# Paged attention of a hybrid decoder: the next sequence's value pages asked for two, two, two and two in the slots of a period instead of two, four and two

## The chip, the core and the metric

One core of a Trainium2 chip runs the whole program. TensorE (PE) multiplies, VectorE (DVE) and ScalarE (ACT) work on the results, GpSimd (POOL) splits weights, SyncE (SP) issues transfers; ScalarE issues transfers too. The transfers run on 16 DMA engines. The metric is the device time of one execution in microseconds (us); lower is better.

## The reference

One inference step of a small decoder: a retention layer with its MLP, then a forgetting-attention layer (FoX) with its MLP, over 512 prompt tokens with 16 meta tokens and over 8 running sequences of 8 new tokens. The change touches only the attention of the 8 running sequences. Each has 1024 past keys and values in 8 pages of 128 rows, found by a page table in a pool in HBM; a page holds 16 heads of 64 floats a row, 512 KB.

```
k_past = cache_k[page_table].reshape(DB, P, FOX_HEADS, FOX_DH)
v_past = cache_v[page_table].reshape(DB, P, FOX_HEADS, FOX_DH)
s = concat(q . k_past, q . k_new) * FOX_SCALE + cum_new[q] - cum_k     # cum: running sum of log forget
p = softmax(where(mask, s, MASK_VALUE))
o = p[..., :P] . v_past + p[..., P:] . v_new
```

## The kernel before, in words

All matrix work is done in float32 or in split float32 (high and low parts). Weights stream through two slots; the layers before and after the attention are bound by PE. The order of work is written out by hand, each engine has its own program, and semaphores join them.

The attention runs from about 1290 to 1557 us of the span. It is one loop over b = 0 to 8 (nine periods), each of four slots i = 0 to 3. A slot of period b does one pair of prompt heads and query block, number j = 4b + i - 2, and a part of the work of sequences b and b - 1:

- Keys. SP asks for key pages (`k_page`, line 683), four transfers of 128 KB a page, into a ring of four buffers (NKS = 4). A buffer is asked for anew when VectorE has turned (transposed) the page in it (line 2390, `turn_page`, into `k_page_t`, four buffers). VectorE turns two pages in every slot, in its program's order, between the row maxima and the sums of the prompt's pair. PE takes two turned pages at a time (`pair_scores`, line 1318).
- Scores and softmax of sequence b - 1 end in slots 0 and 1 of period b: new keys' scores, maxima (line 2397), the exponential on ScalarE (line 1830), transposes on PE (line 1348), and the copies of the transposed probabilities: tokens 512 and on by VectorE, the first 512 and the new ones by ScalarE (lines 1835 and 1838).
- Values. PE multiplies pages 0 to 3 of sequence b - 1 in slot 2 of period b and pages 4 to 7 in slot 3 (`page_values`, line 1363, in page order, 8 instructions a page). It waits there for v_in and then counts v_used. The ring has eight buffers (NVS = 8), the whole of one sequence.
- Requests of values. The first eight pages are asked for by SP. All later ones, 56 of 512 KB, are asked for by ScalarE (line 1846, in `v_next`): it loads the page number from the page table, waits until the page in that buffer has been used, and starts the transfer. Page p of sequence b goes out in period b: pages 0 and 1 in slot 2, pages 2 to 5 in slot 3, pages 6 and 7 in slot 0 of the period after. Each request stands in ScalarE's program behind the activations of its slot, and what follows on ScalarE waits until it is issued.

The names in the rows: `probs_t` is the copy of the prompt pair's transposed probabilities (line 1824, with line 1826 for the meta tokens), which PE's products of line 1293 and 1298 (`values`) wait for; line 1252 is a part of the prompt pair's scores.

Of the kernel before, what the change touches and what calls it, by code (L numbers as in the profile page):

```python
# [206 lines left out]
def program(nc, io):  # L207
    ctx = ExitStack()
    with ctx:
# [354 lines left out]
        def pair_at(b, i):  # L564

            return 4 * b + i - 2

        def live(j):

            return 0 <= j < NPAIR  # L570
# [205 lines left out]
        def _(pe):  # L776
# [123 lines left out]
            def norm_sum(f, n):  # L900

                pe.wait_ge(sq_used, KT * (f + 1))
                a, w = (L0, SL2) if f == 3 else (0, SW)
                for i in range(4):
                    c = slice(a + w * i, a + w * i + w)
                    last = pe.matmul(PS[:, 4 * n.slot + i, HF:HF + w], ck("ones"), RR[:, c], start=False, stop=True,
                                     skip_group_check=True)
                if f == 0:
                    for w, (a, _) in enumerate(WINDOWS):
                        last = pe.matmul(PS[:, 4 * n.slot, HF + SW + w:HF + SW + w + 1], RR[:, a:a + P],  # L910
                                         ck("ones")[:, 0:1], start=False, stop=True, skip_group_check=True)
                last.then_inc(sums_ready, 1)
# [230 lines left out]
            def fox_sums(t):  # L1143

                normed(2)(t)
                if t == KT - 1:
                    pe.wait_ge(sq_used, KT * 3)
                    for hf in range(2):
                        pe.matmul(PS[:, 3 + 4 * hf, 0:HF], ck("ones"), RR[:, HF * hf:HF * hf + HF], start=True, stop=True)
                    for w, (a, _) in enumerate(WINDOWS):  # L1150
                        last = pe.matmul(PS[:, 3, HF + w:HF + w + 1], RR[:, a:a + P], ck("ones")[:, 0:1], start=False,
                                         stop=True, skip_group_check=True)
                    last.then_inc(sums_ready, 1)
# [309 lines left out]
        def _(act):  # L1463
# [343 lines left out]
            def exp(j, par):  # L1807
                n = keys_of(j % 4)
                act.wait_ge(mx_done, 2 * j + (2 if j % 4 == 3 else par + 1))
                act.activation(own_probs(par, n), score_cols(par, n), ACT.Exp, bias=NM[:, par:par + 1],  # L1810
                               accum_out=SM[:, par:par + 1]).then_inc(ex_done, 1)

            def normed_probs(j):
                act.wait_ge(inv_row, j + 1)
                n = keys_of(j % 4)
                for par in range(2):
                    x = own_probs(par, n)
                    act.activation(x, x, ACT.Copy, scale=RM[:, par:par + 1]).then_inc(pn_done, 1)

            def probs_copy(j):  # L1820
                m = P * (j % 4 + 1)
                for par in range(2):
                    act.wait_ge(pt_ready, 3 * j + par + 1)
                    act.activation(PTS[:, par, 0:m], PS[:, 4 + 2 * par, 0:m], ACT.Copy).then_inc(pt_evac, 1)
                act.wait_ge(pt_ready, 3 * j + 3)
                act.activation(PTM[:], PS[0:2 * NMETA, 7, 2 * P:3 * P], ACT.Copy).then_inc(pt_evac, 1)

            def exp_s(b):
                act.wait_ge(smx_done, b + 1)
                act.activation(PB[:], PS[:, 0:3, :].rearrange("p a n -> p (a n)")[:, 0:SK], ACT.Exp, bias=NM[:, 2:3],  # L1830
                               accum_out=SM[:, 2:3]).then_inc(sex_done, 1)

            def probs_copy_s(b):
                act.wait_ge(sp0_ready, b + 1)
                act.activation(PSM[:, 0:4, :], PS[:, 6, :].rearrange("p (t n) -> p t n", t=4), ACT.Copy) \
                    .then_inc(sp0_done, 1)
                act.wait_ge(spn_ready, b + 1)
                act.activation(PSN[:], PS[0:NSAMP, 2, 320:448], ACT.Copy).then_inc(spn_done, 1)

            def v_next(b, pages):  # L1840
                for p in pages:
                    vn = NPAGE * b + p + NVS
                    if 0 <= b < DB - 1:
                        page = act.value_load(PT1[0:1, vn:vn + 1], min_val=0, max_val=io["cache_v"].shape[0] - 1)
                        act.wait_ge(v_used, NPAGE * b + p + 1)
                        act.dma_start(VR[vn % NVS][:], v_pool[bass.ds(page, 1)].rearrange("o k f -> k (o f)")) \
                            .then_inc(v_in[vn % NVS], 16)

            act.wait_ge(k_stored, 48)
            for b in range(DB + 1):  # L1850
                for i in range(4):
                    j = pair_at(b, i)
                    if live(j - 1):
                        probs_copy(j - 1)
                    if live(j):
                        for par in range(2):
                            exp(j, par)
                        normed_probs(j)
                    if i == 0 and b > 0:
                        exp_s(b - 1)  # L1860
                    if i == 1 and b > 0:
                        probs_copy_s(b - 1)
                    if i == 2:
                        v_next(b - 1, (0, 1))
                    if i == 3:
                        v_next(b - 1, (2, 3, 4, 5))
                    if i == 0:
                        v_next(b - 2, (6, 7))
            for dst, src in out_v:
                act.dma_start(dst, src).then_inc(v_stored, 16)  # L1870
# [630 lines left out]
```

## Time and profile before

| what | value |
|---|---|
| time, median of 3 runs (lowest, highest) | 2012.95 us (2012.68, 2015.09) |
| span of the profiled execution (its only time) | 2016.3 us |
| busy share of the span: PE, DVE, ACT, POOL | 96%, 51%, 34%, 22% |
| DMA in the whole span | 239.11 MB, mean 119 GB/s |
| key pages asked for by SP, line 683 | 256 transfers of 128 KB, median 5.9 us to landing |
| value pages asked for by ACT, line 1846 | 56 transfers of 512 KB, median 8.3 us to landing |

The profiled execution is 3.3 us longer than the median of the runs. Times are counted from the start of the span. PE is busy for 96% of the whole, so a reader would look for gains there; the attention is the stretch where it is not. A row of a view of windows gives the length of the stretch, then for each engine its busy time and, in brackets, the instructions begun, the mean granted clock of PE (1.00 is 2.4 GHz, 0.50 is 1.2 GHz), the mean share of the 16 DMA engines that were at work (over 1 where transfers of two queues overlap on an engine), and the rate. A row of a timeline gives start and duration, the engine, line and operation, and in square brackets how long the engine stood idle before it and what ended that.

### The profile page before, as it was taken

To read this page: it belongs to the slowest core of one execution; us is meant where nothing else is said; L and a number is where in the kernel's file an instruction comes from. 1 tells how busy PE (TensorE), PEld (TensorE's weight loads), DVE (VectorE), ACT (ScalarE), POOL (GpSimd) and SP (SyncE) were. 2 spreads that over 40 slices of the span, in tenths; PEclk is the share of its full clock that TensorE was granted. 3 is DMA by queue.
4 is the path that set the end of the run, shared out by engine and by line. 5 is a ranking of instruction groups with operands and counts; after the bars stand their busy time and mean duration, and the time that the engine had idled before them with its cause. 6 is when DMAs were issued, how large, how long until landed. Compare 5 with 4: busy or idle time off the path is not lost.

```text
span 2016.3 us, 35504 instructions
## 1 busy us (share of the span) xinstructions
PE 1926.1 (96%) x14783; PEld 1775.5 (88%) x14783; DVE 1033.0 (51%) x1170; ACT 692.8 (34%) x898; POOL 440.1 (22%) x106
## 2 busy tenths in 40 slices
PE   7999999999999999999999999799997999999998
PEld 6969969969889999999999999655555999999998
DVE  4445245245436865555532535466665466646462
ACT  4132232232224325252531432243545332515241
POOL 2302312312303312121133233000000332121212
PEclk9999999999999999999999999998998999999999
DMA  5341441441243222222232221688998222322231
GB/s 162 126 155 55 137 142 68 137 140 63 101 167 95 84 70 99 84 83 83 98 94 64 65 84 44 206 242 242 286 282 247 85 84 68 101 84 86 80 104 47
DMA packets 197347, 239.11 MB, mean 119 GB/s; under 512 B 16418, under 2 KB 168354, under 8 KB 197026
## 3 DMA queue, kind: packets, MB, share of 16 engines
q1 hardware_dynamic: 175650, 183.27, 30.0%
q10 hardware_dynamic: 21488, 53.46, 8.0%
q8 instruction: 97, 1.59, 0.3%
q0 software_dynamic: 80, 0.52, 0.1%
q14 instruction: 32, 0.26, 0.0%
HBM read 210.77 MB, written 26.12 MB: 117 GB/s over the span
## 4 chain that ended last, share of the span: by engine, by line
PE 64%; issue 16%; DVE 6%; DMA 5%; POOL 4%; ACT 2%; SPq 2%; ACTq 1%; DVEq 0%; POOLq 0%
PE PS L801 12%; PE PS L802 11%; PE PS L803 11%; POOL w_lo L741 4%; PE PS L817 4%; PE PS L819 4%; PE PS L818 4%; DMA k_page<-in_cache_k 3%; PE PS L880 3%; PE PS L881 3%; PE PS L882 3%; SPq L683 1%; DVE k_page_t L2390 1%; PE PS L1363 1%; PE PS L1318 1%
## 5 line engine op out<-in xcount | busy, mean ns | idle before, releaser
L741 POOL TENSOR_TENSOR w_lo<-w_raw,w_hi 128x2048 fp32r<-128x2048 f32 (+2 forms) x101 | 438.9, 4346 | 1545.0 <-ACT w_hi L1468 1545.0
L1468 ACT ACTIVATE w_hi<-w_raw 128x2048 fp32r<-128x2048 f32 (+2 forms) x101 | 178.1, 1764 | 640.8 <-PE PS L803 415.5
L801 PE MATMUL PS<-hidden_hi,w_hi 128*128 128x296 f32 (+1 forms) x1024 | 304.4, 297 | 0.7 <-DVE hidden_tmp L2159 0.6
L803 PE MATMUL PS<-hidden_hi,w_lo 128*128 128x296 f32 (+1 forms) x1024 | 304.7, 298 | 0.0
L802 PE MATMUL PS<-hidden_lo,w_hi 128*128 128x296 f32 (+1 forms) x1024 | 304.2, 297 | 0.0
L801 PE MATMUL PS<-x_hi,w_hi 128*128 128x296 f32 (+1 forms) x896 | 269.9, 301 | 5.7 <-DVE x_lo L1918 2.8
L802 PE MATMUL PS<-x_lo,w_hi 128*128 128x296 f32 (+1 forms) x896 | 268.7, 300 | 0.0
L803 PE MATMUL PS<-x_hi,w_lo 128*128 128x296 f32 (+1 forms) x896 | 268.0, 299 | 0.0
L880 PE MATMUL PS<-w_hi,x_hi 128*128 128x256 f32 x800 | 225.8, 282 | 0.4 <-DVE fox_gate L2311 0.4
L882 PE MATMUL PS<-w_lo,x_hi 128*128 128x256 f32 x800 | 224.8, 281 | 0.0
L881 PE MATMUL PS<-w_hi,x_lo 128*128 128x256 f32 x800 | 224.6, 281 | 0.0
L801 PEld LDWEIGHTS PS<-hidden_hi,w_hi 128*128 128x128 f32 x1024 | 193.1, 189 | 1.6 <-issue 1.0
L802 PEld LDWEIGHTS PS<-hidden_lo,w_hi 128*128 128x128 f32 x1024 | 193.2, 189 | 0.0
L803 PEld LDWEIGHTS PS<-hidden_hi,w_lo 128*128 128x128 f32 x1024 | 192.6, 188 | 0.0
L801 PEld LDWEIGHTS PS<-x_hi,w_hi 128*128 128x128 f32 x896 | 169.6, 189 | 7.4 <-issue 3.5
L802 PEld LDWEIGHTS PS<-x_lo,w_hi 128*128 128x128 f32 x896 | 169.5, 189 | 0.3 <-issue 0.2
L803 PEld LDWEIGHTS PS<-x_hi,w_lo 128*128 128x128 f32 x896 | 169.4, 189 | 0.0
L880 PEld LDWEIGHTS PS<-w_hi,x_hi 128*128 128x128 f32 x800 | 150.5, 188 | 1.1 <-issue 1.0
L882 PEld LDWEIGHTS PS<-w_lo,x_hi 128*128 128x128 f32 x800 | 150.7, 188 | 0.0
L881 PEld LDWEIGHTS PS<-w_hi,x_lo 128*128 128x128 f32 x800 | 150.5, 188 | 0.0
L2159 DVE TENSOR_TENSOR hidden_tmp<-PS,inv_root 128x1184 f32<-128x1184 f32 (+1 forms) x32 | 44.0, 1374 | 178.2 <-PE PS L803 178.0
L1475 ACT ACTIVATE w_hi<-w_raw 128x2048 fp32r<-128x2048 f32 x24 | 46.1, 1919 | 196.6 <-DVE w_raw L2122 196.6
(306 smaller groups left out, 3883.4 us busy)
## 6 DMA issues: line engine op xcount, KB each, us to landing
w_raw<-in_w_mlp_up SPq DMA_DIRECT2D x32, 1024.0 KB, 5.3
w_raw<-in_w_mlp_down SPq DMA_DIRECT2D x32, 1024.0 KB, 5.0
k_page<-in_cache_k SPq DMA_DIRECT2D x256, 128.0 KB, 5.9
v_page<-in_cache_v ACTq DMA_DIRECT2D x56, 512.0 KB, 8.3
w_raw<-in_w_ret_in SPq DMA_DIRECT2D x24, 1024.0 KB, 5.4
sample_state<-in_state_ret SPq DMA_DIRECT2D x32, 512.0 KB, 5.6
out_state_ret_sample<-sample_state ACTq DMA_DIRECT2D x32, 512.0 KB, 4.3
w_raw<-in_w_ret_out SPq DMA_DIRECT2D x16, 512.0 KB, 3.4
```

The source lines that it names most:

```text
L741: pool.tensor_tensor(lo, raw, hi.bitcast(F32), ALU.subtract).then_inc(lo_done, 1)
L801: pe.matmul(o, wh[:, w], xh[:, t, cols], start=(t == 0), stop=False)
L802: pe.matmul(o, wh[:, w], xl[:, t, cols], start=False, stop=False)
L803: last = pe.matmul(o, wl[:, w], xh[:, t, cols], start=False, stop=(t == kt - 1))
L817: pe.matmul(o, wh[:, t], xh[:, t], start=first and t == 0, stop=False, skip_group_check=True)
L818: pe.matmul(o, wh[:, t], xl[:, t], start=False, stop=False, skip_group_check=True)
L819: last = pe.matmul(o, wl[:, t], xh[:, t], start=False, stop=(t == 3), skip_group_check=True)
L880: pe.matmul(o, XH[:, t, tok], wh[:, c], start=start, stop=False, skip_group_check=skip)
L881: pe.matmul(o, XL[:, t, tok], wh[:, c], start=False, stop=False, skip_group_check=skip)
L882: return pe.matmul(o, XH[:, t, tok], wl[:, c], start=False, stop=(t == KT - 1), skip_group_check=skip)
L1468: act.activation(part(WH[n.slot], n, kt), part(WR[n.slot], n, kt), ACT.Copy).then_inc(hi_done, 1)
L1475: act.activation(WH[n.slot][:], WR[n.slot][:], ACT.Copy).then_inc(hi_done, 1)
```

## The change

Inside the loop over b and i, only the place of three of the eight requests changes. Pages 2 and 3 stay in slot 3; pages 4 and 5 go from slot 3 to slot 0 of the next period; pages 6 and 7 go from there to slot 1. The first period in which a request is moved is b = 1 (from its slot 3 on), the last requests now go out in slot 1 of b = 8.

```diff
                     if i == 2:
                         v_next(b - 1, (0, 1))
                     if i == 3:
-                        v_next(b - 1, (2, 3, 4, 5))
+                        v_next(b - 1, (2, 3))
                     if i == 0:
+                        v_next(b - 2, (4, 5))
+                    if i == 1:
                         v_next(b - 2, (6, 7))
```

PE's and SP's programs stay as they are; ScalarE's has the same instructions in another order. The first place is slot 3 of a period, on ScalarE (`v_page_148` to `v_page_155` are the eight buffers of pages 0 to 7; the row of line 1824 opens slot 0):

```order
 L1846 ISA [waits v_used]
 L1846 DMA v_page_151<-in_cache_v 128x1024
-L1844 TENSOR_LOAD page_table_row
-L1844 ISA x2
-L1846 ISA [waits v_used]
-L1846 DMA v_page_152<-in_cache_v 128x1024
-L1844 TENSOR_LOAD page_table_row
-L1844 ISA x2
-L1846 ISA [waits v_used]
-L1846 DMA v_page_153<-in_cache_v 128x1024
 L1824 ACTIVATE probs_t<-PS 128x256 [waits pt_ready] x2
 L1826 ACTIVATE probs_t_meta<-PS 32x128 [waits pt_ready]
```

The requests of pages 4 and 5 no longer stand between that of page 3 and the copies of slot 0. The second place is the end of slot 1 on ScalarE (the rows of lines 1835 and 1838 are the sample's copies, the row of line 1824 opens slot 2):

```order
 L1835 ACTIVATE sample_probs_t<-PS 128x512 [waits sp0_ready]
 L1838 ACTIVATE sample_probs_t_new<-PS 64x128 [waits spn_ready]
+L1844 TENSOR_LOAD page_table_row
+L1844 ISA x2
+L1846 ISA [waits v_used]
+L1846 DMA v_page_154<-in_cache_v 128x1024
+L1844 TENSOR_LOAD page_table_row
+L1844 ISA x2
+L1846 ISA [waits v_used]
+L1846 DMA v_page_155<-in_cache_v 128x1024
 L1824 ACTIVATE probs_t<-PS 128x512 [waits pt_ready] x2
```

The requests of pages 6 and 7 now stand between the sample's copies and the copy of the prompt's probabilities in slot 2.

## Rows read from the trace of the kernel before

**Rows 1.** Windows: six whole periods, the slow one, the shortest, the longest.
```profile
core 0: us, PE busy (x) PEld busy (x) DVE busy (x) ACT busy (x) POOL busy (x), PEclk, DMA share, GB/s
...
1335.10:1521.10 186.00, 168.30 (x1679) 100.58 (x1677) 120.71 (x246) 86.07 (x240) 0.00 (x0) 0.95 1.00 270
...
1364.80:1401.50 36.70, 33.33 (x275) 19.19 (x273) 21.12 (x42) 14.51 (x41) 0.00 (x0) 0.77 0.86 240
1401.50:1430.30 28.80, 27.08 (x286) 16.45 (x288) 19.93 (x42) 14.14 (x41) 0.00 (x0) 1.00 1.02 281
...
1490.10:1521.10 31.00, 26.99 (x285) 16.24 (x282) 19.77 (x42) 14.43 (x41) 0.00 (x0) 1.00 1.04 272
```

**Rows 2.** Waits of VectorE, six periods (total us, times, longest); one in its timeline.
```profile
DVE k_page_t L2390 <- DMA k_page<-in_cache_k: 16.9, 13, 3.0
...
1380.36 1.25 DVE L2390 STREAM_TRANSPOSE k_page_t<-k_page 128x1024 f32<-128x1024 f32 x1 [1.56 <-DMA k_page<-in_cache_k]
```

**Rows 3.** Chain that ended last: start, duration, what.
```profile
1404.02 0.41 PE PS L1252
...
1432.56 0.41 PE PS L1252
...
1441.55 14.96 DMA k_page<-in_cache_k
```

**Rows 4.** Windows: stretches without a hole in the transfers.
```profile
1438.00:1458.00 20.00, 16.74 (x144) 10.41 (x147) 12.91 (x27) 10.05 (x25) 0.00 (x0) 1.00 1.07 297
...
1494.00:1526.00 32.00, 27.99 (x303) 16.63 (x295) 21.21 (x43) 15.22 (x44) 0.00 (x0) 1.00 1.06 275
```

**Rows 5.** Windows of 4 us: the fall of the clock, the hole, a stall.
```profile
1380.00:1384.00 4.00, 2.16 (x5) 1.04 (x7) 1.42 (x2) 1.23 (x5) 0.00 (x0) 0.53 1.07 313
...
1458.00:1462.00 4.00, 4.00 (x66) 2.34 (x58) 3.45 (x7) 1.67 (x6) 0.00 (x0) 1.00 0.70 196
...
1514.00:1518.00 4.00, 1.82 (x16) 1.44 (x15) 1.19 (x2) 2.48 (x6) 0.00 (x0) 1.00 1.13 242
```

**Rows 6.** Value pages asked for in slot 2, from 1460.8: landing.
```profile
DMA to landing us min/median/max: 5.3/6.3/7.4
```

**Rows 7.** Value pages asked for in slot 3, from 1496.3: landing.
```profile
DMA to landing us min/median/max: 8.6/10.4/11.8
```

**Rows 8.** Timeline of ScalarE, slots 0 and 1 into slot 2.
```profile
1416.04 1.17 ACT L1830 ACTIVATE sample_probs<-PS,neg_max 128x1088 f32<-128x1088 f32 x1 [0.31 <-DVE neg_max L2397]
1416.73 0.37 ACTq L1846 DMA_DIRECT2D v_page<-in_cache_v  x1
...
1417.82 0.38 ACTq L1846 DMA_DIRECT2D v_page<-in_cache_v  x1
1418.24 0.87 ACT L1824 ACTIVATE probs_t<-PS 128x384 f32<-128x384 f32 x2 [0.94 <-PE PS L1285]
...
1425.80 0.26 ACT L1838 ACTIVATE sample_probs_t_new<-PS 64x128 f32<-64x128 f32 x1
1427.20 1.09 ACT L1824 ACTIVATE probs_t<-PS 128x512 f32<-128x512 f32 x2 [1.15 <-PE PS L1281]
1428.17 0.25 ACT L1826 ACTIVATE probs_t_meta<-PS 32x128 f32<-32x128 f32 x1
```

**Rows 9.** Timeline of PE, slot 2 of the same period.
```profile
1429.50 0.48 PE L1293 MATMUL PS<-probs_t_meta,meta_v_by_head 32*128 32x128 f32 x2
```

**Rows 10.** Value pages of slot 3, last period, no keys beside them: landing.
```profile
DMA to landing us min/median/max: 4.1/4.5/4.9
```

**Rows 11.** Timelines of ScalarE and PE: the last period.
```profile
1544.11 0.26 ACT L1838 ACTIVATE sample_probs_t_new<-PS 64x128 f32<-64x128 f32 x1
...
1549.50 2.80 PE L1363 MATMUL PS<-v_page,sample_probs_t 128*32 128x256 f32 x48
```

**Rows 12.** Timelines of ScalarE and PE: slot 1, next slot 3.
```profile
1484.69 0.26 ACT L1838 ACTIVATE sample_probs_t_new<-PS 64x128 f32<-64x128 f32 x1
...
1495.90 1.07 PE L1363 MATMUL PS<-v_page,sample_probs_t 128*32 128x256 f32 x16
```

## The prediction, made before the changed kernel was run

> **What bounds the kernel now.** I read the busy slices of the page first, to find the stretch that the change lies in: the paged attention, from about 1290 to 1557 us. I then cut that stretch into periods, at the request for value pages 0 and 1 in each slot 2. Six whole periods take 186.0 us together [rows 1]. One of them takes 36.7 us at a mean granted clock of 0.77; the other five share 149.3 us, 29.9 us each, from 28.8 to 31.0. In all of them the share of the 16 DMA engines stands near 1, so transfers are the scarce thing, and PE, at 27 us busy of 29, is next to them.
>
> The waits of VectorE say which transfer is late: over these six periods it stood 16.9 us, in 13 waits, before a key page that it had to turn [rows 2]. No PE wait for a value page is listed. The chain of waits says what that costs. From one PE scores row (L1252, slot 3) to the same place a period later it runs 1432.56 - 1404.02 = 28.5 us through PE and DVE without a long step on a transfer [rows 3]; in the next period a key page that took 14.96 us stands in it. So 28.5 us is what the work needs where keys come in time. The five periods at full clock lie 149.3 - 5 x 28.5 = 6.8 us above it.
>
> Key pages are late behind a full set of engines, not because the engines cannot carry the period. A period moves 16 pages of 512 KB, 8.39 MB. In stretches without a hole it went at 297 and at 275 GB/s [rows 4], which is 28.2 and 30.5 us a period. And there is a hole: from 1458 to 1462 the DMA share is 0.70 at 196 GB/s [rows 5], when the value pages of slots 3 and 0 have landed, those of slot 2 are not asked for yet, and only four key pages can be under way. Before it the values of six or eight pages lie in front of the keys; in it the engines lack work.
>
> **The change, part by part.** *Slot 3 loses two requests.* Four requests there keep landings at 8.6 to 11.8 us, against 5.3 to 7.4 us for a pair in slot 2 [rows 6, 7]. Two fewer put 1.05 MB less in front of the key pages of slots 0 and 1, at the rates above 3.5 to 3.8 us of transfer, which is more than the longest single key wait of 3.0 us [rows 2]. ScalarE also leaves slot 3 some 2.2 us earlier (the gap from one activation to the next with two requests between them, worked out below). No one gains by that: its next work is the copy of the prompt's probabilities, and PE uses that copy at the end of slot 0, behind key scores that wait for VectorE. I take 0; the bounds are 0 and a gain of 2.2 us a period.
>
> *Slot 0 keeps two requests, for other pages.* Cost 0: the same two instructions in the same place.
>
> *Slot 1 gains two requests*, behind the two copies of the sample's probabilities. Slot 0 shows what two requests cost ScalarE: from the start of the activation that they follow (1416.04) to the next one (1418.24) 2.20 us [rows 8]. In slot 1 the last copy starts at 1425.80, and the next activation, at 1427.20 today, cannot start before 1428.00: 0.80 us later. Queued behind the requests are that copy (1.09 us) and the small one of 0.25 us, so they end near 1429.3; PE's product that waits for both starts at 1429.50 [rows 9]. The cover is 0.2 us. I take 0, and keep as bounds a gain of 0 and a loss of 0.6 us a period (0.8 less 0.2), 3.6 us over six. The waits on v_used that move along are for pages read a slot or more earlier, so they hold nothing.
>
> *What lies on the path.* The pair of slot 1 would go out near 1455, just ahead of the hole, and the hole is filled. The period then ends at the later of two limits: 28.5 us of work, or the transfers without a hole, 28.2 to 30.5 us. Those two ends are the bounds; I take 29.1 us, between the middle of the transfer bounds (29.35) and the work's 28.5, because a hole-free period also mixes keys and values evenly. Five periods: 149.3 - 5 x 29.1 = 3.8 us. The sixth, the one at 0.77, has 1.56 us of the key waits [rows 2]; of the 15.3 us in the other five some 6.8 us showed on the path, 45%, so 0.7 us here. Together 4.5 us. The bounds: at 28.5 us 6.8 + 0.7 = 7.5 us gained, at 30.5 us 3.2 us lost.
>
> *The end.* In the last period pages 6 and 7 are asked for in slot 1, not slot 0. The copy that the requests follow starts at 1544.11, so with slot 0's offsets (0.69 and 1.78 us [rows 8]) they go out at 1544.8 and 1545.9. With no keys beside them four requests landed in 4.1 to 4.9 us [rows 10]: 1549.7 and 1550.8 at the latest. PE takes pages 2 to 7 in 2.80 us from 1549.50 [rows 11], page 6 at 1551.4 and page 7 at 1551.8. In time by 1 us: 0, and at worst 1.5 us.
>
> Sum: 4.5 us off. The profiled execution spans 2016.3 us; by the sum it would be 2011.8. That execution is 3.3 us over the median of the runs, 2012.95, so the forecast is 2012.95 - 4.5 = **2008.5 us**.
>
> **The rivals.** *The clock comes back as well.* In the period of 36.7 us the granted clock fell to 0.5 (1.2 GHz) near 1380, within the stall of that 1.56 us key wait [rows 2, 5]; against a period of 29.1 us that cost 7.6 us, of which 0.7 is counted above. If the fall goes with the stall, 6.9 us more are gained: 2012.95 - 11.4 = 2001.5. Against it: the stall of 1514 to 1518, where PE was busy 1.82 us of 4 and the clock stayed at 1.00 [rows 5], so a key wait alone does not bring a fall. The Trainium skill (TensorE: Matmul & The Clock Gate, HAM oscillation) has waits for DMA throw the engine back to the lower clock; by that rule this rival is the forecast, and the trace agrees in one stall and not in the other.
>
> *Nothing is gained.* The bytes of a period stay, the engines are near 1.0 throughout, and if even mixing runs at the lower rate, 281 GB/s, a period takes 29.9 us as today: 2011 to 2015. For it speaks that the hole is only some 0.3 x 4 = 1.2 us; against it, that keys are late in the slots after the long burst and not elsewhere. The Trainium skill (DMA: Bandwidth & Descriptors, Issuing engines are not separate DMA queues) says that transfers asked for from different engines interleave on the same 16 engines and that only issue time can be saved; by that rule this rival holds, and the share above 1.0 in rows 4 agrees with it.
>
> *Pages 6 and 7 come late: slower.* Requested after the copy that starts at 1484.69, they would go out at 1485.4 and 1486.5; PE reads the pair from 1495.90 on, page 7 at 1496.4 [rows 12], before the scores of the next slot. That leaves 10.5 and 9.9 us, where today they have a whole slot more. At the 11.8 us of rows 7 page 7 would be 1.9 us late in each of six periods, 11.4 us in all, which takes the gain of 4.5 and adds 6.9: 2020. It decides from a landing of 9.9 us on, and turns the sign from 9.9 + 4.5 / 6 = 10.7 us on. Pairs landed in 5.3 to 7.4 us [rows 6], which speaks against it.
>
> **How the numbers follow.** Forecast 0.42, with its own range of 2005.5 to 2012; the clock as well 0.20; nothing gained 0.23; late pages 0.15. The range of eight in ten goes from 2001 to 2016: it holds the forecast, most of the clock's case, all of no gain, and the milder late pages. About 0.2%, 4 us, is what a measurement here can tell from no change. Faster than 2008.9 takes 0.20 of the clock's case, some 0.26 of the forecast's and 0.02 of the rest: 0.48. Slower than 2017 takes most of the late pages and of a second fall of the clock, 0.14. The rest is 0.38.
>
> **What would show it.** Right: VectorE's waits for key pages between slot 2 of b=1 and slot 2 of b=7 fall from 16.9 us to under 6; full-clock periods lie at 28.5 to 29.5 us; the share holds above 0.9 around the requests of slot 2. PE's first product with the small copy in slot 2 moves by under 0.3 us. Wrong: key waits stay over 12 us with the same period (no gain), PE waits for v_page in slot 3 (late pages), or a granted clock of 0.5 in another period than before.

## The result and the profile after

The changed kernel is slower: 2019.91 us median (2013.77 to 2031.43, six runs) against 2012.82 us (2009.78 to 2015.09, six runs), ratio 1.006 with a 95% interval of 1.0036 to 1.0083. The prediction was 2008.5 us, range 2001 to 2016: wrong in sign. A second set of runs, below, gave 1.0084 (1.0052 to 1.0117).

The profiled execution of the changed kernel, 2016.84 us, is one of its fastest; its span of 2015.0 us is even below that of before, since the attention began some 9 us earlier in it. So the stage is compared, not the span. First the windows over six periods (requests of slot 2 to requests of slot 2), then three single periods: one without a long key wait, one with, and one with none at all:

```profile
core 0: us, PE busy (x) PEld busy (x) DVE busy (x) ACT busy (x) POOL busy (x), PEclk, DMA share, GB/s
1326.30:1518.40 192.10, 173.22 (x1665) 103.11 (x1661) 122.49 (x246) 85.79 (x240) 0.00 (x0) 0.92 1.02 262
...
1423.00:1452.00 29.00, 27.28 (x283) 16.52 (x285) 19.89 (x42) 14.17 (x41) 0.00 (x0) 1.00 0.98 250
1452.00:1485.70 33.70, 28.08 (x281) 16.84 (x281) 21.12 (x42) 14.27 (x41) 0.00 (x0) 0.95 1.02 259
1485.70:1518.40 32.70, 30.98 (x278) 18.31 (x276) 20.46 (x42) 14.44 (x41) 0.00 (x0) 0.84 1.08 277
```

192.1 us against 186.0 [rows 1], at a mean granted clock of 0.92 against 0.95. In the period shown below no hole is left in front of the requests of slot 2 (share 0.98 from 1448, 1.08 from 1452), as forecast; but holes of 0.70 and 0.67 stand in windows of 4 us from 1380 and from 1480, a slot earlier, ahead of the requests of slot 1. The rate of 262 GB/s against 270 is the same bytes in more time. VectorE's waits for key pages in these periods, and PE's waits from 1320 to 1550 for `o_tok`, the output of a sample:

```profile
DVE k_page_t L2392 <- DMA k_page<-in_cache_k: 14.0, 8, 3.8
```
```profile
PE PS L1377 <- DVE o_tok L2409: 9.0, 3, 4.4
```

The sum of the key waits has fallen little (16.9 us before [rows 2]). But there are 8 instead of 13, and PE now stands for up to 4.4 us in one piece at line 1377, the transpose of a sample's output. Before, its waits for turned keys were these, none over 1.5 us; its longest stand inside the periods was 2.7 us at line 1285, for the gate of the prompt's pair (`fox_gate`), which VectorE writes behind a late key:

```profile
PE PS L1318 <- DVE k_page_t L2390: 4.9, 4, 1.5
...
1381.84 0.40 PE L1285 MATMUL PS<-c_keep_sb,probs 128*32 128x128 f32 x1 [2.71 <-DVE fox_gate L2383]
```

How the new stand comes about shows in one period. The requests of ScalarE there:

```profile
1447.21 0.35 ACTq L1846 DMA_DIRECT2D v_page<-in_cache_v  x1
...
1448.28 0.35 ACTq L1846 DMA_DIRECT2D v_page<-in_cache_v  x1
1451.99 1.42 ACTq L1846 DMA_DIRECT2D v_page<-in_cache_v  x2
1460.07 1.44 ACTq L1846 DMA_DIRECT2D v_page<-in_cache_v  x2
```

The requests at the end of slot 1 (from 1447.21) and those of slot 2 (from 1451.99) lie 4.8 us apart: four value pages, 2.1 MB, go out within 6.2 us. The burst of slot 3 has been moved, not spread. Of the five such neighbours in these periods four lie 4.8 us apart, and three of these are followed by late keys in slot 3; the fifth, at 1423, lies 7.3 us apart and is followed by none. The key pages asked for at the same time feed the turns of slot 3; the slowest of the quarters asked for from 1447 to 1451 took 12.5 us. What follows, on VectorE and PE, and then on the chain of waits:

```profile
1463.15 1.25 DVE L2392 STREAM_TRANSPOSE k_page_t<-k_page 128x1024 f32<-128x1024 f32 x1 [3.80 <-DMA k_page<-in_cache_k]
...
1465.93 0.42 PE L1377 MATMUL PS<-c_keep_sb,o_tok 128*64 128x128 f32 x1 [4.36 <-DVE o_tok L2409]
```
```profile
1450.66 12.47 DMA k_page<-in_cache_k
...
1465.10 0.49 DVE o_tok L2408
1465.93 0.42 PE PS L1377
```

VectorE's program has the output of the sample behind the second turn of slot 3, and PE's has the transpose of that output early in slot 0, so the late key stops both. Right behind it the clock falls, as windows of 4 us show:

```profile
1460.00:1464.00 4.00, 1.57 (x9) 1.02 (x9) 0.85 (x1) 0.32 (x1) 0.00 (x0) 1.00 1.10 261
1464.00:1468.00 4.00, 2.07 (x14) 1.41 (x18) 3.80 (x13) 1.15 (x4) 0.00 (x0) 0.73 1.06 272
```

This fall is short: the granted clock is 0.50 for 3.4 us. The same holds behind the other long stands at line 1377: 3.2 us in this profile, 4.1 and 5.0 us in that of the second set, each followed by 3.4 us at half clock. The long stretches at half clock lie elsewhere. Inside the periods of the two profiles they last 10.2, 10.2, 13.7 and 20.5 us, and begin at, or some 5 us after, PE's wait at line 1285, which took 1.6, 1.1, 2.3 and 3.4 us there. So did the one of 17 us of the kernel before, at the 2.7 us shown above. The period from 1485.7 has such a stretch (clock 0.84) with no late key at all.

From the first sample exponential to the first product after the attention (begin of `fox_y_hi`), the stage of the kernel before, of the changed one, and of the changed one in the profile of its second set:

```profile
1320.50:1556.50 236.00, 209.61 (x2091) 125.62 (x2089) 147.46 (x301) 109.08 (x298) 4.52 (x1) 0.95 0.93 260
```
```profile
1311.70:1554.30 242.60, 216.80 (x2092) 130.06 (x2090) 147.83 (x301) 108.78 (x298) 4.53 (x1) 0.92 0.95 254
```
```profile
1315.00:1567.10 252.10, 222.76 (x2090) 132.81 (x2089) 147.41 (x301) 109.01 (x298) 4.53 (x1) 0.89 0.92 243
```

Longer by 6.6 and 16.1 us, at clocks of 0.92 and 0.89. PE does the same instructions in 7.2 and 13.2 us more. Its idle time, length less busy time, is 26.4 us before and 25.8 and 29.3 us after: the waiting was regrouped more than it was lengthened, and most of what the stage lost is the same work at a lower clock.

### The profile page after: what moved, and what is told of

It is laid out like the page before. It is cut to its first block, busy times and chain, and to the rows that moved or that the text cites. A ratio compares the mean times of both kernels' runs of the same rounds, so it can differ in the third digit from the quotient of the medians.

```text
span 2015.0 us, 35504 instructions
## 1 busy us (share of the span) xinstructions
PE 1932.3 (96%) x14783; PEld 1779.4 (88%) x14783; DVE 1033.1 (51%) x1170; ACT 692.4 (34%) x898; POOL 440.3 (22%) x106
## 4 chain that ended last, share of the span: by engine, by line
PE 65%; issue 17%; DVE 6%; POOL 4%; DMA 3%; ACT 2%; SPq 2%; ACTq 1%; DVEq 0%; POOLq 0%
PE PS L801 11%; PE PS L802 11%; PE PS L803 11%; POOL w_lo L741 4%; PE PS L817 4%; PE PS L819 4%; PE PS L818 4%; PE PS L880 3%; PE PS L881 3%; PE PS L882 3%; DMA k_page<-in_cache_k 2%; PE PS L1318 1%; DVE k_page_t L2392 1%; PE PS L1363 1%; SPq L683 1%
```

## The experiments

All ratios are to the kernel before in the same set of runs. The mean clock is that of a kernel's runs, the granted clock of PE over the span; that of the kernel before was 0.984 to 0.986 in every set of experiments. A stage clock is that of one profiled execution. Four theories are set against each other: by the place theory the loss comes by late keys in slot 3, which hold the sample's output; by the rate theory by more bursts of values; by the ScalarE theory by the two requests in front of the copy of slot 2; by the clock theory by time at half clock.

**The changed kernel again**, without an edit. 

> The changed kernel once more, beside fresh runs of the kernel before. Clock theory (the loss is time at half clock, set off by key waits that lengthen PE's idle stretch of slots 3 and 0): ratio 1.003 to 1.009, mean granted clock of its runs 0.004 to 0.008 under that of the runs of the kernel before, and time falling by 13 to 20 us per 0.01 of clock. If the loss were transfer time alone, the clocks would agree within 0.002.

1.0084 (1.0052 to 1.0117). Mean clock 0.9781 in 7 runs against 0.9857 in 24 of before; within its own runs time falls 17.7 us for each 0.01 of clock, within those of before 12.6. By these slopes the difference of 0.0076 goes with 10 to 13 us of the 17.4 us between the means (an estimate). Loss and low clock go together; which brings which is for the next ones.

**Half of the value bytes.** The same edit (shortened here) in the kernel before and in the changed one; it leaves out the other 64 rows of each page:

```diff
-act.dma_start(VR[vn % NVS][:], v_pool[bass.ds(page, 1)]...)
+act.dma_start(VR[vn % NVS][0:64], v_pool[bass.ds(page, 1), 0:64]...)
```

> The kernel before, but every value page that ScalarE asks for brings only the first 64 of its 128 rows (the other rows stay from the first pages), so values move half the bytes. Base for the next run. All theories: key pages are no longer late (VectorE waits under 4 us for them in the six periods against 16.9), periods near 28.5 us, 2000 to 2009 us, unless the clock falls more often.

> The changed kernel with the same half pages (first 64 rows only). If the loss comes by the key pages (place theory: a late key page in slot 3 holds the output that PE waits for; rate theory: dearer bytes), it is gone: within 0.2% of the kernel before with half pages, PE's wait for o_tok under 2 us. If it comes by the order on ScalarE (two requests ahead of the probability copy of slot 2), it stays: 5 to 8 us slower than that kernel.

2007.66 us (0.999, 0.9965 to 1.0015) and 2003.15 us (0.9966, 0.9944 to 0.9987): with the changed order the half pages are not slower but, if anything, faster. No key wait is left in either, and in the second six periods in a row take 28.5 us. So the loss needs the full value bytes and the late keys that come with them; the order on ScalarE alone makes none, and that theory fell. What the key waits of the kernel before cost in all is not settled. By the medians it is 2.5 us, with an interval from 7 us gained to 3 us lost. The stage of the profiled execution is 7.8 us shorter than before (236.0 us), and 7.0 us of that is PE's idle time, 19.4 us against 26.4:

```profile
1316.00:1544.20 228.20, 208.81 (x2091) 125.19 (x2089) 148.43 (x301) 108.01 (x297) 4.52 (x1) 0.96 0.85 205
```

The clock falls here too: for 10.2 us from 1351 in this profile and from 1490 in that of the changed order, with no late key and no stand over 1.1 us in front. So late keys are not the only thing that brings a fall.

**Parts of the change and other orders.** Only the places of the requests differ.

```diff
 # pages asked for in slots 2 | 3 | 0 | 1
-  0,1 | 2,3,4,5 | 6,7 | -        (before; the change: 0,1 | 2,3 | 4,5 | 6,7)
+  0,1 | 2,3,4,5 | -   | 6,7      (first)
+  0,1 | 2,3     | 4,5,6,7 | -    (second)
+  -   | 0,1,2,3 | 4,5 | 6,7      (third)
+  0,1,2,3 | -   | 4,5 | 6,7      (fourth)
```

First: 

> Only pages 6 and 7 are moved, from slot 0 to slot 1; pages 2 to 5 stay in slot 3 (two, four, none, two in slots 2, 3, 0, 1). Place theory (requests at the end of slot 1 and in slot 2 lie within 6 us of each other and in front of the key pages that VectorE turns in slot 3, where its output of the sample stands behind the turn and PE waits for it): as slow as the full change, 2016 to 2022 us, with PE waiting for o_tok (line 1377) over 6 us inside the periods. Rate theory (the more separate bursts of values, the dearer each byte; three bursts here as before): 2010 to 2015 us, DMA rate over the six periods near 270 GB/s. ScalarE theory (two requests ahead of the probability copy of slot 2 delay PE): 2016 to 2022 us, with PE's line 1293 late in slot 2.

1.0069 (1.0047 to 1.0091), PE's wait for o_tok 6.9 us in 3: as slow as the whole change, by pages 6 and 7 alone.

Second: 

> Only pages 4 and 5 are moved, from slot 3 to slot 0, which now asks for four (two, two, four, none). Place theory: nothing is asked for in slot 1, so the keys of slot 3 come in time; key waits sit in slots 0 to 2 as before: 2009 to 2015 us, PE's wait for o_tok under 3 us. Rate theory: three bursts, as before: 2010 to 2015 us and 270 GB/s. ScalarE theory: slot 1 is as before, 2010 to 2014 us.

1.011 (1.0086 to 1.0134): missed by all. No key wait is left, and no wait for o_tok inside the periods; four requests in slot 0 hold ScalarE's copy, and PE waits for it in slot 1, where the clock falls too (stage clock 0.86):

```profile
PE PS L1267 <- ACT probs_t L1824: 7.5, 6, 1.8
```

Third: 

> Slot 2 asks for none, slot 3 for pages 0 to 3, slot 0 for 4 and 5, slot 1 for 6 and 7. Place theory: the requests of slot 1 stay where the change put them, but those of slot 2 no longer follow within 6 us, so the keys of slot 3 have two pages in front of them and not four: 2010 to 2016 us, PE's wait for o_tok under 4 us. Rate theory: three bursts: 2010 to 2015 us. ScalarE theory: slot 1 as in the change, 2016 to 2022 us.

0.9994 (0.9974 to 1.0015), mean clock 0.9856: the loss is gone though slot 1 asks for its two pages as in the change. PE still waits 4.9 us for o_tok, more than forecast, but in 4 pieces of 1.8 us at most. The longest key wait is 1.7 us:

```profile
DVE k_page_t L2390 <- DMA k_page<-in_cache_k: 12.2, 15, 1.7
```

With 12.2 us of key waits in these short pieces PE's idle time in the stage is 19.7 us, hardly more than the 19.4 us without any key wait. So by these two profiles short waits of VectorE are nearly free for PE.

Fourth: 

> Slot 2 asks for pages 0 to 3, slot 3 for none, slot 0 for 4 and 5, slot 1 for 6 and 7: six pages between the end of slot 1 and slot 2, where the change has four and the order none, four, two, two has two. Place theory (pages asked for in slots 1 and 2 stand before the keys that slot 3 turns): key waits in slot 3 and the waits for o_tok at least as long as with the change, 9 to 16 us, 2018 to 2028 us. If slot 1's requests alone made the loss: 2016 to 2022 us. If the number of bursts made it (three here): as before, 2008 to 2013 us.

1.0078 (1.0051 to 1.0105): the time as the place theory had it, its means not: 4.0 us of key waits, no wait for o_tok inside the periods, and a stage clock of 0.85. That the keys come in time because PE works at half clock for so long is likely, but not shown. What started the falls there is open. The three orders with requests in both slot 1 and slot 2 (the change, first, fourth) are slow, and so, by another wait, is the second; three bursts alone (before, first, third) go both ways, so the rate theory fell as well.

**The output ahead of the late turn**, in the changed kernel, on VectorE (shortened):

```diff
+if i == 3: gated(j - 1); output_s(b - 1)
 turn_page(NPAGE * b + 2 * i + 1)
-if i == 3: gated(j - 1); output_s(b - 1)
```

> The changed kernel, with VectorE's second key turn of slot 3 moved behind the gate of the prompt's pair and the output of the sample, so that a late key page no longer holds the output. Place theory: PE's wait for o_tok (10.8 us in four times before) falls under 3 us and at least half of the loss comes back, 2012 to 2017 us; part may return as a wait for the turned page itself (line 1318). Rate theory and ScalarE theory: the order on VectorE does not touch the transfers or ScalarE, so the loss stays: 2017 to 2023 us.

1.0095 (1.0076 to 1.0113): missed. The wait for o_tok inside the periods is gone, but a period without waits takes 29.4 us in place of 28.5, and the stage clock is 0.84. The edit adds its own delay, so it doesn't tell the place. But it shows a larger loss of clock than the change itself with no stand over 2.4 us.

**PE's idle stretch filled** with repeats of transposes that it does anyway, in the time of its wait at line 1285 (shortened):

```diff
-for kb in range(j % 4 + 1):                                       # probs_t, second head
+for kb in [x for _ in range(1 + par * again) for x in range(j % 4 + 1)]:   # again = 3 in slot 1
```

In the kernel before: 

> The kernel before, with the transposes of the second head's probabilities in slot 1 done four times in place of once (nine more matmuls of some 0.13 us a period, same result), in the 1.1 us in which PE waits there for the gate. Clock theory (the idle stretch of slots 0 and 1 decides whether PE's clock falls): less than 25 us at half clock in the attention (41 before) and 2003 to 2010 us. Without it: 2011 to 2016 us, the added work costs up to 0.2 us a period.

0.9973 (0.9952 to 0.9994), 2004.93 us, mean clock 0.9877 against 0.9841; the stage's clock is 0.98, and more instructions take less time:

```profile
1317.80:1545.80 228.00, 212.34 (x2163) 130.77 (x2161) 146.52 (x301) 108.82 (x298) 4.53 (x1) 0.98 0.96 269
```

The granted clock stays at 1.00 through all its periods from 1320 to 1528, though VectorE's key waits, 13.8 us in 12 with 2.7 us at most, are much as without the fill.

In the changed kernel: 

> The changed kernel with the same nine more transposes. Clock theory: half clock in the attention falls from 58 us to under 40, and half of the loss comes back, 2010 to 2016 us. Place theory without the clock (the late output alone makes the loss): the waits for o_tok stay at 8 to 12 us and the time at 2017 to 2023 us.

1.0006 (0.9982 to 1.003), mean clock 0.9849 against 0.978 without the fill, while PE's waits for o_tok stay (8.8 us in 3). The one stretch of 10 us at half clock left in its periods begins 5 us after a wait of 2.0 us at line 1285. So a large part of the loss goes by the clock. Not all of it: with the fill in both, the changed kernel stands at 1.0006 against 0.9973. These 0.33%, just at the edge of noise, are about half of the loss without the fill.

In the third order above: 

> None, four, two, two together with the nine more transposes of slot 1: the order with the shortest key waits and the filled idle stretch. Clock theory: both hold, faster than the kernel before by 4 to 10 us (ratio 0.995 to 0.998) with under 30 us at half clock in the attention. If the fill gained by chance: ratio 0.998 to 1.001.

0.9998 (0.9982 to 1.0014), mean clock 0.9868: missed. Why it gains nothing is not shown: without the fill this order had the same mean clock, 0.9856, as the kernel before, which did gain. The two intervals overlap, so the size of that gain is uncertain too. The kernel before with the fill stays the fastest version with whole pages by its ratio.

With one long burst (0 to 5 in slot 3, 6 and 7 in slot 0): 

> All six of pages 0 to 5 in slot 3, 6 and 7 in slot 0, none in slots 2 and 1, with the nine more transposes. Place theory: no values between slots 1 and 2, so no wait for o_tok over 1 us; the long burst makes keys late in slots 0 and 1 instead, 12 to 22 us in all, which costs less: ratio 0.995 to 1.000. If any late key costs the same wherever it falls: 1.000 to 1.006.

1.0043 (1.0025 to 1.006): no late key at all, but six requests hold ScalarE 5.9 us in slot 3, and every period takes 30.8 us or more. Missed.

**Stalls made by hand**, in the kernel before with half value pages (2007.66 us, measured in another set of runs), so that no key is late and the transfers are the same in number and size:

```diff
+for _ in range(3 if kn in (23, 39, 55) else 0):   # slot 3; the second: (19, 35, 51), slot 1
+    do(dve.transpose(KP[:, kn % NTURN], ...))      # the turn that follows, done before it
 dve.transpose(KP[:, kn % NTURN], ...).then_inc(k_turned, 1)
```

Slot 3: 

> The kernel before with half value pages (no key page is late in it, 2007.7 us), with a stall made by hand: in the slots 3 of b = 2, 4 and 6 VectorE turns the second key page four times in place of once, 3.7 us more in front of the output of the sample, 11 us in the three. Values move as in that base; only half the value rows are read. Place theory: PE waits for o_tok 3 to 4.5 us each time, as with the change, and the stall is paid in full, with the clock on top: 2017 to 2032 us, mean clock 0.003 or more under the base's 0.984. If a stall of VectorE costs the same wherever it falls: equal to the next run.

Slot 1: 

> The same base and the same three stalls of 3.7 us, but on the second key page of the slots 1 of b = 2, 4 and 6, where the long key waits of the kernel before lay. Place theory: about half is hidden, and the clock falls less: 2010 to 2017 us, at least 6 us under the run with the stalls in slot 3. If place does not matter: within 3 us of that run.

2014.76 (1.0021, 1.0001 to 1.0042) and 2013.61 us (1.0028, 1.0006 to 1.005). PE waits for o_tok 8.6 us in 3, in sum as with the change but 2.9 us at most, and in slot 1 for the turned page 7.5 us in 3. By the medians both cost 6 to 7 us, against a base with an interval of 5 us to either side: that slot 3 pays more than slot 1, as the place theory had it, does not show in the time. It shows in the clock: the mean is 0.9815 with the stalls in slot 3 and 0.9845 with those in slot 1.

Slot 3 with the fill: 

> The stalls in slot 3 again, with the nine more transposes in slot 1 of every period. Clock theory: the stalls still cost their 11 us, but less is lost to the clock: 5 to 12 us under the run with the stalls in slot 3 and no fill, mean clock at least 0.003 over it. Without a clock effect: within 3 us of that run.

2015.26 us (1.0034, 1.0011 to 1.0057), mean clock 0.9831 against 0.9815: no gain, missed.

Then the length, with one turn more (1.24 us) in every slot 3, and with four turns more (5.0 us) in four of them (`range(1 if kn % 8 == 7 else 0)`, `range(4 if kn in (15, 31, 39, 55) else 0)`).

Short: 

> The kernel before with half value pages again, and eight stalls of one key turn (1.24 us) in front of the output of slot 3, one in every period: 9.9 us of VectorE in short pieces. Length theory (a short wait fits into the slack of a slot, a long one leaves PE idle in one piece, is paid in full and brings the clock down): under 0.4 us of time for each us of stall, 2004 to 2011 us, mean clock within 0.002 of the base's 0.984. If a stall costs the same per us whatever its length, as the stalls of 3.7 us did (0.6): 2012 to 2015 us.

Long: 

> The same base with four stalls of four key turns (5.0 us each, 19.8 us in all) in front of the output of slot 3, in b = 1, 3, 4 and 6: as many and as long as the stalls of the changed kernel. Length theory: PE idle 4 us in one piece, over 1 us of time for each us of stall: 2026 to 2038 us, mean clock 0.980 or less, as in the changed kernel. If the cost per us stays at 0.6: 2017 to 2022 us; then the changed kernel's low clock has a further cause.

2006.89 us (0.9991, 0.9971 to 1.0012; clock 0.9855) and 2026.85 us (1.0089, 1.0061 to 1.0116; clock 0.9787). PE's waits, short and long:

```profile
PE PS L1377 <- DVE o_tok L2409: 3.8, 8, 1.5
```
```profile
PE PS L1377 <- DVE o_tok L2409: 16.7, 4, 4.2
```

9.9 us of VectorE's time in pieces of 1.24 us cost nothing that shows; 11 us in pieces of 3.7 us cost some 7; 19.8 us in pieces of 5.0 us cost 19, and bring time and clock to those of the changed kernel in its second set. So in these stalls a us costs more, the longer the piece it comes in; the long ones are also the larger sum. And they are more than what they stand for: PE waits 16.7 us for o_tok in 4 there, against 9.0 in 3 and 9.1 in 2 in the changed kernel. Its low clock therefore has a further cause. A late key in slot 0, which holds the gate of line 1285, is the candidate of the profiles above; no stall was made by hand there.

## Why the prediction was wrong

**What bounds it: right.** The 28.5 us of a period without late keys stood in the changed kernel with half pages, six times in a row. One reading beside it was too even: the share of the DMA engines was near 1 in five of the six periods of before, and 0.86 in the slow one [rows 1].

**"The pair of slot 1 would go out near 1455, just ahead of the hole, and the hole is filled": the step that failed.** The hole in front of slot 2 was filled, but a request there stands 4.8 us before that of slot 2. The prediction set the pages per slot against the time per slot, and did not look at the times of the requests: the end of slot 1 and slot 2 are neighbours, slots 3 and 0 are 8 to 13 us apart in this trace. So the pair of slot 2 landed, in the period shown, not in 5.3 to 7.4 us [rows 6] but in 9.1 to 10.7. The six periods took 192.1 us where the sum gives 181.5, 186.0 less 4.5. Moving pages 6 and 7 alone gave the whole loss, and moving the pair of slot 2 to slot 3 took the loss off again.

**"6.8 us showed on the path, 45%": a measure that did not carry over.** It spread the cost evenly over the waits. But the waits of the third order cost PE next to nothing in short pieces, while with much the same sum as before (14.0 us for 16.9) the changed kernel's longest key wait grew from 3.0 to 3.8 us and PE's longest stand from 2.7 to 4.4. Whether 4.5 us were there to win at all is open: without any key wait the kernel before is 2.5 us faster by the medians of the runs, 7.8 us by one profile of each.

**The clock: the largest term, and with the wrong sign.** The prediction had one fall that might go, and no term for new ones. It took the stall at 1514 [rows 5] as a sign that a key wait alone leaves the clock alone; but there PE stood twice, 0.9 and 1.4 us, and at the fall of 1380 once, 2.7 us, not the 1.56 us of the key wait. Of the 17 us between the means of the second set 10 to 13 go with the clock, PE's busy time in the stage rose by 7.2 and 13.2 us, and filling PE's idle time brought the changed kernel back to 1.0006. The Trainium skill (TensorE: Matmul & The Clock Gate, HAM oscillation) says that waits on DMA throw the engine back to its lower clock; the hand-made long stalls agree, with 0.9787 against 0.984, the short ones not, with 0.9855.

**Slot 3, slot 0, slot 1 on ScalarE at 0: right**, as far as the half pages can show it. **The end and late value pages:** no wait of PE for a value page in the changed kernel, as forecast; that rival's 2020 us meets the measured 2019.9 by luck, for its mechanism did not occur. **No gain by equal bytes:** wrong for this order, right for none, four, two, two.

Open: how much of a long stall is its own length and how much the clock (the fill gave back 11 to 16 us in the changed kernel, by its two ratios, and none of the hand-made stalls), and what starts each fall: in the second and fourth orders, with the output first, and in periods with no late key.

## What to carry to other kernels

Spread requests by the times at which they are issued, read from the trace, not by the program's slots; here two small bursts 4.8 us apart acted as one. When a wait is moved or shortened, look at the pieces in which TensorE then stands, at the stretch behind each, and at the granted clock there; neither the sum of the waits nor the longest of them told the loss here. Before a rival is priced by one fall of the clock, take the mean clock of several runs.

## What the runs showed of the hardware that was not expected

The same kernel's time moved by 16 to 23 us within a set of 17 runs or more, and with it the mean granted clock: 9 to 20 us for each 0.01, by kernel and set. Nine more matmuls a period in idle time made a kernel faster by 0.27% (0.06 to 0.48), with the clock at 1.00 through the periods of its profile.
